# Moving the norm factor of an MLP into its up phase, the residual into accumulating transfers, and the last norm into token halves

## The reference

```python
hm = rmsnorm(x, p['g_mlp'])
x = x + jnp.square(jax.nn.relu(hm @ p['w_up'])) @ p['w_down']
...
y = rmsnorm(x, g_final)       # over the 2048 channels of each token
```

## Time and profile before

| | |
|---|---|
| median of 3 runs | 3149.82 us (3148.88 to 3153.22) |
| profiled execution, its own time | 3146.49 us |
| its span, first to last instruction | 3144.5 us |
| PE busy | 2983.5 us, 95% of the span |
| DVE busy | 2037.4 us, 65% |
| ACT busy | 1099.5 us, 35% |
| POOL busy | 645.9 us, 21% |
| mean granted PE clock | 0.978 of full |

### The profile page before, as it was taken

How to read it: one execution, slowest core, us unless ns; L and a number is a source line. 1 busy time by engine, 2 the same in 40 slices (tenths; PEclk the granted TensorE clock), 3 DMA queues, 4 the chain that set the end, 5 groups by cost and what they waited for, 6 DMA issues and landing times.

```text
span 3144.5 us, 62566 instructions
## 1 busy us (share of the span) xinstructions
PE 2983.5 (95%) x27548; PEld 2913.6 (93%) x27548; DVE 2037.4 (65%) x2325; ACT 1099.5 (35%) x1252; POOL 645.9 (21%) x264
## 2 busy tenths in 40 slices
PE   8999999999978699999999899999999999999994
PEld 8999999999978699988799899999999999999994
DVE  6416974443766622311322888888887888898987
ACT  5432122223212222311132455555555333333331
POOL 6964433333300044322144000000000000000000
PEclk9999999999989899999999999999999999999996
DMA  8763523323210133455453256666668555555541
GB/s 272 221 191 95 101 95 119 95 89 95 76 71 3 64 104 119 163 200 200 133 197 120 91 182 205 203 203 198 194 194 288 193 192 201 203 203 194 198 152 61
DMA packets 230894, 485.85 MB, mean 155 GB/s; under 512 B 25056, under 2 KB 132832, under 8 KB 219744
## 3 DMA queue, kind: packets, MB, share of 16 engines
q1 hardware_dynamic: 128880, 321.79, 31.5%
q10 hardware_dynamic: 101744, 160.07, 14.7%
HBM read 396.51 MB, written 85.30 MB: 153 GB/s over the span
## 4 chain that ended last, share of the span: by engine, by line
PE 24%; DVE 14%; issue 6%; ACT 4%; DMA 2%; ACTq 0%; DVEq 0%; POOL 0%; POOLq 0%
PE mp L1810 10%; PE gp L1810 8%; DVE sums L2358 5%; PE gp L1694 5%; DVE lo L2367 3%; ACT hi L2030 2%; DMA u_scratch<-ul 1%; ACT work L2062 1%; DVE ul L2409 1%; DVE work L2400 1%; DVE work L2394 1%; ACT uh L2071 0%; PE gp L1743 0%; DVE work L2402 0%; DVE work L2404 0%
## 5 line engine op out<-in xcount | busy, mean ns | idle before, releaser
L1694 PE MATMUL gp<-xh,hi 128*128 128x260 f32 x3072 | 878.8, 286 | 13.0 <-DVE xl L2212 12.0
L1694 PE MATMUL gp<-xh,lo 128*128 128x260 f32 x3072 | 870.4, 283 | 0.0
L1694 PE MATMUL gp<-xl,hi 128*128 128x260 f32 x3072 | 867.8, 282 | 0.0
L1667 POOL TENSOR_TENSOR lo<-raw,hi 128x1024 fp32r<-128x1024 f32 x256 | 638.5, 2503 | 1093.9 <-ACT hi L1893 1073.2
L1893 ACT ACTIVATE hi<-raw 128x1024 fp32r<-128x1024 f32 x260 | 274.5, 1059 | 955.3 <-PE gp L1694 878.0
L1694 PEld LDWEIGHTS gp<-xh,hi 128*128 128x128 f32 x3072 | 581.0, 189 | 25.2 <-issue 20.1
L1694 PEld LDWEIGHTS gp<-xl,hi 128*128 128x128 f32 x3072 | 580.6, 189 | 0.6
L1694 PEld LDWEIGHTS gp<-xh,lo 128*128 128x128 f32 x3072 | 580.6, 189 | 0.0
L2030 ACT ACTIVATE hi<-sums 128x1024 fp32r<-128x1024 f32 x256 | 271.1, 1059 | 398.1 <-DVE sums L2358 296.2
L1810 PE MATMUL mp<-ub,hi 128*128 128x260 f32 x2048 | 378.5, 285 | 8.7 <-DVE lo L2367 3.1
L1810 PE MATMUL mp<-xs,hi 128*128 128x260 f32 x2048 | 375.9, 284 | 2.9 <-DVE work L2379 1.8
(11 more groups left out here) (388 smaller groups left out, 4683.4 us busy)
## 6 DMA issues: line engine op xcount, KB each, us to landing
raw<-in_w_up SPq DMA_DIRECT2D x128, 512.0 KB, 5.3
raw<-in_w_down SPq DMA_DIRECT2D x128, 512.0 KB, 4.6
ub<-u_scratch ACTq DMA_DIRECT2D x56, 1040.0 KB, 14.4
raw<-in_w_in SPq DMA_DIRECT2D x100, 512.0 KB, 3.6
u_scratch<-uh ACTq DMA_DIRECT2D x32, 910.0 KB, 8.1
u_scratch<-ul ACTq DMA_DIRECT2D x32, 910.0 KB, 9.3
raw<-in_w_k SPq DMA_DIRECT2D x32, 512.0 KB, 4.5
raw<-in_w_v SPq DMA_DIRECT2D x32, 512.0 KB, 4.4
```

The costliest lines, as they stand in the source:

```text
L1667: nc.gpsimd.tensor_tensor(lo[:, s, :], raw[:, s, :], hi[:, s, :].bitcast(F32), ALU.subtract).then_inc(lo_ready, 1)
L1694: last = nc.tensor.matmul(gp[:, par, h, 0:c1 - c0], w, m[:, c0:c1], start=a, stop=b)
```

## The change

Four things. (1) The factor r itself, not r², is made before the up phase needs it (ACT takes two roots, DVE one reciprocal of 520 columns), and DVE multiplies it in where it also takes relu: one `scalar_tensor_tensor` over 1040 columns, `relu_scale`, placed in DVE's list behind low part n+2 of the next group. ACT keeps only the square. The hidden quarters are laid out in another order so that each meets its token half. (2) The residual is added into D by four POOL transfers that accumulate, each after the first down group of its quad; D's next use waits for it. (3) The last norm is split: ACT squares D and multiplies the gain in, for quads 0 to 2 behind the next group's last high part; the last quad goes by token halves, half 1 (ready three products early) before half 0. (4) r² and its way to DRAM and back, the X_f loads and the sixteen multiplications fall away; eight multiplications of 1040 columns and eight stores of half size stand at the end.

```diff
@@ tiles @@
-KIND = (1, 3, 5, 4, 2, 0, 6)
+KIND = (2, 4, 5, 3, 1, 0, 6)
-        rs2 = wk(OFF_Y + 7800, T)
+        rsw = wk(OFF_Y + 7800, 2, H2)
@@ POOL @@
-                if dq == DQ - 1:
-                    pool.wait_ge(S("r_moved"), 16)
                 nc.gpsimd.memset(D[:, dq, :, :, :, :], 0.0).then_inc(S("m_zero"), 1)
+            for dq in range(DQ):
+                pool.wait_ge(m_evac, ev(UPG + dq, "d_fin"))
+                pool.wait_ge(S(f"x_spilled{dq}"), 32)
+                if dq:
+                    pool.wait_ge(S("x_added"), 16 * dq)
+                pool.dma_start(D[:, dq, :, :, :, :].rearrange("p q m t n -> p (q m) (t n)"), xt[:, 4 * dq:4 * dq + 4, :],
+                               accum_op=ALU.add, max_dma_last_dim=4 * T).then_inc(S("x_added"), 16)
@@ PE @@
-            pe.wait_ge(S("acc"), at("acc", "f") + 1)
-            pe.wait_ge(m_evac, ev(GROUPS - 1, "d_fin"))
-            for h, (c0, c1) in enumerate(two):
-                last = nc.tensor.matmul(mp[:, h, 0:H2], ones[:, :], acc_f[:, c0:c1], start=True, stop=True)
+            for h in (1, 0):
+                pe.wait_ge(S("acc"), at("acc", "f") + 2 - h)
+                if h == 1:
+                    pe.wait_ge(m_evac, ev(GROUPS - 1, "c_fin"))
+                nc.tensor.matmul(mp[:, h, 0:H2], ones[:, :], acc_f[:, h, :], start=True, stop=True).then_inc(S("ss"), 1)
@@ ACT @@
-            def relu_square(g):
+            def hid_square(g):
                 z = g % 2
-                act.wait_ge(m_evac, ev(g, "cross"))
-                act.wait_ge(S("m_a"), g + 1)
-                nc.scalar.activation(F[:, z, 0:4, :], F[:, z, 0:4, :], ACT.Relu).then_inc(S("m_sq"), 1)
-                act.wait_ge(S("m_sq"), 2 * g + 1)
+                act.wait_ge(S("m_relu"), g + 1)
                 nc.scalar.activation(F[:, z, 0:4, :], F[:, z, 0:4, :], ACT.Square).then_inc(S("m_sq"), 1)
...
             act.wait_ge(S("ss"), 4)
+            act.wait_ge(S("x_spilled3"), 32)
+            for h in range(2):
+                nc.scalar.activation(rsw[:, 1 - h, :], mp[:, 2 + h, 0:H2], ACT.Sqrt, scale=1.0 / DM, bias=epst[:, 0:1]).then_inc(S("root"), 1)
             x_hi(6)
...
-                if g == GROUPS - DQ:
-                    act.wait_ge(unit_done, U_MLP + n)
-                    act.dma_start(rs2_f, rt).then_inc(S("r_moved"), 16)
-                    for c in range(4):
-                        act.wait_ge(S(f"x_spilled{c}"), 32)
-                        act.dma_start(X_f[:, 4 * c:4 * c + 4, :], xt[:, 4 * c:4 * c + 4, :]).then_inc(S(f"x_loaded{c}"), 16)
...
                 if g > GROUPS - DQ:
                     dq = g - 1 - (GROUPS - DQ)
-                    act.wait_ge(S("m_final"), 2 * dq + 1)
-                    nc.scalar.activation(sq_f, X_f[:, 4 * dq:4 * dq + 4, :], ACT.Square).then_inc(S("sq"), 1)
+                    act.wait_ge(m_evac, ev(g - 1, "d_fin"))
+                    if dq:
+                        act.wait_ge(S("m_final"), dq)
+                    nc.scalar.activation(sq_f, D[:, dq, :, :, :, :].rearrange("p q m t n -> p q m (t n)"), ACT.Square).then_inc(S("sq"), 1)
+                    act.wait_ge(S("sq"), at("sq", "f") + dq + 1)
+                    for k in range(4 * dq, 4 * dq + 4):
+                        nc.scalar.activation(D_tile(k), D_tile(k), ACT.Copy, scale=pr("g_final", k)).then_inc(S("m_gf"), 1)
...
+            for t, what in ((1, "c_fin"), (0, "d_fin")):
+                act.wait_ge(m_evac, ev(GROUPS - 1, what))
+                nc.scalar.activation(sq_l[:, t, :, :, :], D[:, last, :, :, t, :], ACT.Square).then_inc(S("sq"), 1)
+                act.wait_ge(S("sq"), at("sq", "f") + DQ + 1 - t)
+                for k in range(4 * last, KT):
+                    nc.scalar.activation(D_tile(k)[:, H2 * t:H2 * t + H2], ..., ACT.Copy, scale=pr("g_final", k)).then_inc(S("m_gf"), 1)
+                act.wait_ge(S("ss"), 6 - t)
+                nc.scalar.activation(rstd_f[:, t, :], mp[:, t, 0:H2], ACT.Sqrt, scale=1.0 / DM, bias=epst[:, 0:1]).then_inc(S("root"), 1)
@@ DVE @@
+            def relu_scale(g):
+                z = g % 2
+                dve.wait_ge(m_evac, ev(g, "cross"))
+                dve.wait_ge(S("m_a"), g + 1)
+                f4 = F[:, z, 0:4, :].rearrange("p (a b) n -> p a (b n)", a=2)
+                V.scalar_tensor_tensor(out=f4, in0=f4, scalar=0.0, in1=rsw.rearrange("p b n -> p (b n)").unsqueeze(1).broadcast_to([P, 2, T]),
+                                       op0=ALU.max, op1=ALU.mult).then_inc(S("m_relu"), 1)
...
+                elif g < UPG + 2 * DQ:
+                    dve.wait_ge(S("x_added"), 16 * (g - UPG - DQ + 1))
...
+            def finish_half(t):
+                dve.wait_ge(S("root"), 7 - t)
+                lane.done(V.reciprocal(rstd_f[:, t, :], rstd_f[:, t, :]))
+                for c in range(DQ):
+                    dve.wait_ge(S("m_gf"), 4 * (c + 1) if c < DQ - 1 else 4 * DQ + 4 * (1 - t))
+                    rows = D[:, c, :, :, t, :].rearrange("p q m n -> p (q m) n")
+                    V.tensor_tensor(rows, rows, rstd_f[:, t:t + 1, :].broadcast_to([P, 4, H2]), ALU.mult).then_inc(S("y_final"), 1)
...
-            dve.wait_ge(S("ss"), 4)
-            dve.wait_ge(S("x_spilled3"), 32)
-            V.tensor_scalar(halves(rs2), mp[:, 2:4, 0:H2], 1.0 / DM, EPS, ALU.mult, ALU.add).then_inc(S("m_var"), 1)
+            dve.wait_ge(S("root"), 5)
+            lane.done(V.reciprocal(rsw, rsw))
             for g in range(1, UPG):
                 n = SEVEN * g
                 m_sum(g, 4)
                 c_cross(g - 1)
                 m_low(n + 2)
+                relu_scale(g - 1)
                 m_low(n + 3)
                 m_low(n + 4)
                 u_sums(g - 1)
-                if 1 <= g <= 4:
-                    dve.wait_ge(S("m_var"), 1)
-                    q = slice((g - 1) * (T // 4), g * (T // 4))
-                    V.reciprocal(rs2[:, q], rs2[:, q]).then_inc(S("m_inv"), 1)
...
                 m_low(n + 8)
+                if g == GROUPS - 1:
+                    add_squares(DQ - 2)
+                    add_half(1)
                 a_fin(g)
                 m_sum(g + 1, 3)
-                if g > GROUPS - DQ:
-                    finish_quads(g - 1 - (GROUPS - DQ))
+                if g > GROUPS - DQ and g < GROUPS - 1:
                     add_squares(g - 1 - (GROUPS - DQ))
             d_fin(GROUPS - 1)
-            finish_quads(DQ - 1)
-            add_squares(DQ - 1)
-            dve.wait_ge(S("root"), 5)
-            lane.done(V.reciprocal(rstd_f, rstd_f))
-            for k in range(KT):
-                V.scalar_tensor_tensor(out=X_f[:, k, :], in0=X_f[:, k, :], scalar=pr("g_final", k), in1=rstd_f, ...)
+            add_half(0)
+            finish_half(1)
+            finish_half(0)
```

More of the change, by code:

```diff
@@ L225, in program @@
         ud = nc.dram_tensor("u_scratch", [FB, P, SEVEN, 2, QT, H2], F32, kind="Internal").ap()
-        rt = nc.dram_tensor("r_scratch", [P, T], F32, kind="Internal").ap()
         def wk(off, *dims):
@@ L1498, in program @@
         D = wk(OFF_Y, KT * T).rearrange("p (d q m t n) -> p d q m t n", d=DQ, q=2, m=2, t=2)
[L1499 to L1502 removed]
+        acc_f, rstd_f = wk(0, 2, H2), wk(T, 2, H2)
+        sq_f = wk(2 * T, 2, 2, 2 * H2)
+        sq_l = wk(6 * T, 2, 2, 2, H2)
+        s_f = wk(10 * T, 2, T)
         u_landed = [S(f"u_landed{b}") for b in range(2)]
@@ L1824, in seven_up @@
                     if i == 1 and g == 1:
-                        pe.wait_ge(S("m_var"), 1)
+                        pe.wait_ge(S("root"), 5)
                     if i == 1 and g >= 2:
@@ L2095, in last_copy @@
                     act.wait_ge(S(f"x_spilled{g}"), 32)
-                nc.scalar.activation(F[:, g % 2, 2, :], pa(g % 2), ACT.Copy).then_inc(S("m_a"), 1)
+                nc.scalar.activation(F[:, g % 2, 3, :], pa(g % 2), ACT.Copy).then_inc(S("m_a"), 1)
             def u_load(f, i):
@@ L2170, in _ @@
                     dq = g - 1 - (GROUPS - DQ)
-                    act.wait_ge(S("m_final"), 2 * dq + 1)
-                    nc.scalar.activation(sq_f, X_f[:, 4 * dq:4 * dq + 4, :], ACT.Square).then_inc(S("sq"), 1)
-            act.wait_ge(S("m_final"), 2 * DQ - 1)
-            nc.scalar.activation(sq_f, X_f[:, 4 * DQ - 4:4 * DQ, :], ACT.Square).then_inc(S("sq"), 1)
-            act.wait_ge(S("ss"), 5)
-            for h, (c0, c1) in enumerate(two):
-                nc.scalar.activation(rstd_f[:, c0:c1], mp[:, h, 0:H2], ACT.Sqrt, scale=1.0 / DM, bias=epst[:, 0:1]).then_inc(S("root"), 1)
@@ new lines, in _ @@
+                    act.wait_ge(S("sq"), at("sq", "f") + dq + 1)
+                    for k in range(4 * dq, 4 * dq + 4):
+                        nc.scalar.activation(D_tile(k), D_tile(k), ACT.Copy, scale=pr("g_final", k)).then_inc(S("m_gf"), 1)
+            last = DQ - 1
+            for t, what in ((1, "c_fin"), (0, "d_fin")):
[3 more added lines that the diff above has]
+                for k in range(4 * last, KT):
```

(28 more changed lines are left out.)

31 lines of the change are left out of this document (5 added, 26 removed).

## The result

The changed kernel takes 3154.2 us (median of 18 runs, 3151.2 to 3158.6), the kernel before, run beside it, 3149.2 us (18 runs, 3142.1 to 3153.2). The ratio is 1.0021, 95% interval 1.0014 to 1.0028: slower, by 5.0 us between the medians and by 6.6 us by the ratio, which is small but clear of the noise. 3153.5 us had been forecast. The two profiled executions differ by 8.0 us in their spans, 3144.5 and 3152.5, and this is where the 8.0 are. Stages go from mark to mark on DVE and PE, so that they add up.

A forecast was written before the change was run, and what follows sets the result against it. It took a DVE-ACT ring as long as PE's work to bound the up phase, and DVE the end. Terms +33.4, +4.0, +0.6, +0.5, -16.7, -18.1 sum to +3.7 us: median 3153.5 us, own range 3147 to 3159, 8-in-10 range 3141 to 3168.

The forecast's parts named there:

- the two large sums: Whole kernel: costs of +33.4, +4.0, +0.6 and +0.5 us against savings of -16.7 and -18.1 us, cancelling to +3.7.
- within 0.2%: Whole kernel: the forecast's case of a time within 0.2% of no change, chance 0.55 of the forecast's 0.75.
- The ring: Up phase: DVE and ACT loop from one `c_cross` to the next grows from 20.21 to 21.39 us, +33.4 us.
- Rival 3: Up phase: DVE's 1.2 us gap takes up the relu pass, +33.4 becomes 0, 3120 us; chance 0.10.
- The stop of PE: Up phase: from the second group on PE stops about 1.15 us per group, waiting for `w_c`.
- The low clock at the start: Start of up phase: PE's clock low behind its longer stop, +0.5 us, between 0 and 1.7.
- The start: Start of up phase: ACT's table load and roots and DVE's reciprocal of 520 columns delay the first `c_cross` by 4.0 us.
- The down phase: Down phase: the four POOL transfers finish before D's next use, so they cost 0 us.
- perhaps three times: Down phase: upper bound of 28 us for an accumulating transfer, against 9.5 us for a plain reload.
- The second rival: Down phase: accumulating transfers late or holding up loads, `c_mid` waits; +5 to +15 us, worst +40; chance 0.07.
- The last groups: Last down groups: without two DVE passes and the wait for ACT's square, PE hardly stops; -16.7 us.
- the tail: Behind the last product: 39.2 us shrink to 21.1, since half 1 is summed earlier; -18.1 us.

## Why the prediction was right, and where not

**The sum.** The net result was forecast at +3.7 us. It was measured at +5.0 between the medians, +6.6 by the ratio and +8.0 between the two profiles. The direction of each large term was right, and the two large sums did cancel as forecast; but 0.16% to 0.21% is at the edge of the "within 0.2%" that was given 0.55. That the median came within 0.7 us of 3153.5 is partly luck: stage by stage the forecast was 4.3 us short, 3.5 of it in the down phase.

**The ring: right, by its mechanism and size.** The step that decides, that DVE's idle 2 us per round are links of a ring and not room, was tried from three sides. Less in the ring gave rounds of 20.37, more in it 22.52 or more, and DVE's pass taken out with the relu back on ACT 20.20. Rival 3, that the gap takes the pass in, was false for the order that the change chose and true for the order one place earlier. The gap could take the work, if the pass stood ahead of the low part: the square is then released early, and the low part is worked while ACT squares. The prediction had this in its sentence "the pass is ahead of the gap", but did not draw from it that the order alone was worth 29 us.

**The stop of PE: right in kind.** It was 0.90 to 0.96 us, 1.15 had been forecast. The low clock at the start, for which +0.5 was added, costs nothing: the round behind it takes 21.38 us as all others do, so it is hidden in the longer ring.

**The start** is +4.06 for +4.0, by the rows that were named: 1.14 of waiting for ACT behind the table load and the roots, and 3.40 for 0.69 on DVE.

**The down phase is the term that failed:** 0 was forecast, 3.5 us were measured. "So 0 at both ends" came from asking only whether the transfers are in time for their own reader. They were: DVE never waited for one. What was not asked is whom they delay. The fourth was issued where seven products of the next block and the weights are loaded, took 22.8 us instead of about 10, and weights came 1.5 us later: +1.8 us in that interval against the kernel before, gone when it is moved. The "perhaps three times" that the prediction set as a bound on the time to landing came true in another place, in the engines' time (an estimated 6.5 us against 2.4). Another +1.6 is PE's low clock behind the turn, for which the sum had no term, and which four kernels with all the transfers do not have. The second rival had named the cause (holding up the loads that share the engines), but only as a wait of 5 us and more.

The Trainium skill (SBUF — State Buffer, Who interferes with whom) says that DVE passes in a 2-port mode starve such transfers, and that sums of two tensors were not seen to, for a reason that it infers. The trace agrees with the second half so far as it goes: beside a DVE that is busy with such sums, three of the four landed after 8.7 to 10.2 us, as the plain reload did, and the fourth, which was late beside the same sums, landed after 11.1 us when it was moved to a place with fewer loads.

**The last groups and the tail: right**, -16.2 and -18.1. The prediction named two causes for the old last groups, the two passes and the wait for ACT's square. Putting the passes back shows 13.3 us of the 23.4 by which the last three intervals had shrunk; the share of the waits was not tested. The tail's chain was worked out to 21.1 us and measured at 21.2.
